# Hybrid retention / sparse attention / MoE layer on one core: the last expert's down product in its own banks, four of nine final tiles summed by TensorE

## What is computed

```python
def expert_block(args):
    tok, e = args
    xb = h[tok]
    hid = jax.nn.silu(xb @ w_gate[e]) * (xb @ w_up[e])
    return hid @ w_down[e]
...
x = x + hier_moe(...)          # each frame: gate_0 * row_0 + gate_1 * row_1
y = rmsnorm(x, g_final)
```

## Time and profile before

| | us |
|---|---|
| median of three runs | 1272.99 (1272.86 to 1273.10) |
| the profiled execution | 1269.63 |
| its span | 1267.8 |
| TensorE busy | 1122.5 (89%) |
| VectorE busy | 866.8 (68%) |
| ScalarE busy | 690.8 (54%) |
| GpSimd busy | 244.4 (19%) |

### The profile page before, as it was taken

How to read it: one execution, slowest core, us unless ns; L and a number is a source line. 1 busy time by engine, 2 the same in 40 slices (tenths; PEclk the granted TensorE clock), 3 DMA queues, 4 the chain that set the end, 5 groups by cost and what they waited for, 6 DMA issues and landing times.

```text
span 1267.8 us, 18011 instructions
## 1 busy us (share of the span) xinstructions
PE 1122.5 (89%) x6433; PEld 938.5 (74%) x6433; DVE 866.8 (68%) x1771; ACT 690.8 (54%) x1183; POOL 244.4 (19%) x276
## 2 busy tenths in 40 slices
PE   5998889999999899999999789997699999999920
PEld 4985477887878897888988468885578888888810
DVE  6529868787878777433242533356899999999847
ACT  6347578686868333243433432113378888888622
POOL 1320033324342200000000000000233433433213
PEclk8999999999999999999999899998799999999965
DMA  8352030404030232432423625103599999999656
GB/s 275 45 118 26 29 96 1 109 1 108 1 86 1 57 106 82 109 87 79 118 59 102 222 65 198 50 34 133 216 402 400 392 388 397 386 398 391 243 214 254
DMA packets 129536, 205.35 MB, mean 162 GB/s; under 512 B 17396, under 2 KB 102804, under 8 KB 117156
## 3 DMA queue, kind: packets, MB, share of 16 engines
q1 hardware_dynamic: 114852, 177.61, 40.4%
q0 software_dynamic: 12864, 21.02, 5.3%
q10 hardware_dynamic: 1728, 5.51, 1.1%
HBM read 182.03 MB, written 34.37 MB: 171 GB/s over the span
## 4 chain that ended last, share of the span: by engine, by line
PE 76%; DVE 13%; ACT 3%; issue 3%; DMA 2%; SPq 1%; POOL 0%; DVEq 0%; POOLq 0%; ACTq 0%
PE psum L2186 5%; PE psum L2188 5%; PE psum L2187 5%; PE psum L2461 4%; PE psum L2459 4%; PE psum L2460 4%; DVE place L1440 3%; PE psum L2334 3%; PE psum L2336 3%; PE psum L2335 3%; PE psum L2159 3%; PE psum L2161 2%; PE psum L2160 2%; PE psum L2476 2%; PE psum L2478 2%
## 5 line engine op out<-in xcount | busy, mean ns | idle before, releaser
L1858 DVE TENSOR_TENSOR place<-place,place 128x2048 fp32r<-128x2048 f32 x64 | 146.2, 2286 | 8.4 <-ACT place L1246 8.4
L1071 ACT ACTIVATE place<-place,place 128x768 uint8<-128x768 f32 (+3 forms) x128 | 125.5, 983 | 6.8 <-DVE place L1471 6.8
L2186 PE MATMUL psum<-place,place 128*128 128x512 f32 x288 | 123.7, 430 | 3.0 <-DVE place L1427 2.9
L1246 ACT CAST place<-place 128x2048 fp32r<-128x2048 f32 x64 | 122.2, 1912 | 0.0
L2188 PE MATMUL psum<-place,place 128*128 128x512 f32 x288 | 114.2, 397 | 0.0
L2187 PE MATMUL psum<-place,place 128*128 128x512 f32 x288 | 113.9, 396 | 0.0
L2459 PE MATMUL psum<-place,place 128*128 128x512 f32 x256 | 107.1, 418 | 0.0
L2461 PE MATMUL psum<-place,place 128*128 128x512 f32 x256 | 102.2, 399 | 0.0
L2460 PE MATMUL psum<-place,place 128*128 128x512 f32 x256 | 101.2, 395 | 0.0
L2159 PE MATMUL psum<-place,place 128*128 128x256 f32 x288 | 86.9, 302 | 3.5 <-ACT place L1093 3.5
L882 POOL TENSOR_TENSOR place<-place,place 128x1 f32<-128x1 f32 x9 | 5.1, 566 | 428.4 <-DVE place L1818 428.4
(11 more groups left out here) (324 smaller groups left out, 3111.1 us busy)
## 6 DMA issues: line engine op xcount, KB each, us to landing
place<-in_w_gate SPq DMA_DIRECT2D x32, 1024.0 KB
place<-in_w_up SPq DMA_DIRECT2D x32, 1024.0 KB
place<-in_w_down SPq DMA_DIRECT2D x32, 1024.0 KB, 10.7
place<-in_w_in SPq DMA_DIRECT2D x28, 512.0 KB, 6.4
place<-expert_out SPq DMA_DIRECT2D x9, 1024.0 KB, 13.0
place<-in_cache_attn_k SPq DMA_DIRECT2D x32, 256.0 KB, 3.2
place<-in_cache_attn_v SPq DMA_DIRECT2D x32, 256.0 KB, 3.4
place<-in_x_prompt SPq DMA_DIRECT2D x3, 1536.0 KB, 6.8
```

What stands on the lines that cost most here:

```text
L1071: last = nc.scalar.activation(reached[j], score[j], ACT.Sign, bias=pivot.bitcast(F32)[:, j:j + 1], scale=-1.0, accum_out=minus[:, j - BY_A ...
L1246: nc.scalar.copy(w_gu_hi[e % 2][:, :, ks, :], w_gu[e % 3][:, :, ks, :]).then_inc(w_hi_done, 1)
L1858: nc.vector.tensor_tensor(w_gu_lo[e % 3][:, :, ks, :], w_gu[e % 3][:, :, ks, :], w_gu_hi[e % 2][:, :, ks, :].bitcast(F32), ALU.subtract).t ...
L2186: nc.tensor.matmul(bank(4 + b), hT_hi[:, k, rows], w_hi[:, k, :], start=k == 0, stop=False)
```

## The change

The last expert's `down` writes banks 2 and 3 and no longer waits for `rows_out(30)`. Its weights are rounded and their remainder is formed one turn ahead on both engines. TensorE does the transposes `hidden(31)` between the two halves of `down(30)`. Then four of the nine final tiles (1, 3, 5, 7) are summed by TensorE in PSUM: identity times `x1` plus two products with diagonal matrices that hold the gates, which ScalarE writes beforehand. The tiles are finished in the order 0, 2, 1, 4, 3, 6, 5, 7, 8, and the normed tile is written over the first half of its own loaded rows instead of one of three buffers. The loads still go out in the order 0 to 8.

```diff
+ON_PE, LAST_ORDER = (1, 3, 5, 7), (0, 2, 1, 4, 3, 6, 5, 7, 8)
...
-        out_rows = [take(D) for _ in range(3)]
+        gate_diagonal = [[place(xT_at + 3 * D + P * (2 * n + j), P) for j in range(2)] for n in range(len(ON_PE))]
+        out_rows = [rows[:, 0, :] for rows in y_in]
...
+        def down_bank(e):
+
+            return 6 if e < NE - 1 else 2
...
+        def x2_after(x):
+
+            return sum(0 if t in ON_PE else 2 for t in LAST_ORDER[:x + 1])
...
-                nc.scalar.copy(y_rows[e % 2][:, 0:512], bank(6)).then_inc(y_act, 1)
+                nc.scalar.copy(y_rows[e % 2][:, 0:512], bank(down_bank(e))).then_inc(y_act, 1)
...
             for e in range(NE):
                 if e + 1 < NE:
                     rows_hi(e + 1)
+                else:
+                    down_hi(e)
...
                 gate_silu(e)
-                down_hi(e)
+                if e + 1 < NE:
+                    down_hi(e)
+                else:
+                    hidden_hi(e)
                 if e >= 1:
                     rows_out(e - 1)
-            hidden_hi(NE - 1)
             rows_out(NE - 1)
+            for n, t in enumerate(ON_PE):
+                for j in range(2):
+                    nc.scalar.activation(gate_diagonal[n][j], ident, ACT.Copy, scale=gates[:, j, t:t + 1]).then_inc(mix_hi_done, 1)
...
+            for x in range(T + 1):
+                if x < T:
+                    t = LAST_ORDER[x]
+                    if t in ON_PE:
+                        act.wait_ge(wo_ps, T + ON_PE.index(t) + 1)
+                        rows = bank(2 * ON_PE.index(t), 0, D)
+                    else:
+                        act.wait_ge(x2_done, x2_after(x))
+                        rows = x1[:, t, :]
+                    act.wait_ge(ssq_done, 2 * T + x)
+                    nc.scalar.activation(squared, rows, ACT.Square, accum_out=ssq7[:, x:x + 1]).then_inc(ssq_done, 1)
+                if x >= 1:
+                    t = LAST_ORDER[x - 1]
+                    act.wait_ge(out_done, x)
+                    act.dma_start(y_p[t * P:(t + 1) * P, :] if t < TP else y_s, out_rows[t]).then_inc(y7_out[(x - 1) % 3], 16)
...
-                nc.vector.tensor_scalar(y_rows[e % 2][:, 512:D], bank(7), 1.0, None, ALU.mult).then_inc(y_dve, 1)
+                nc.vector.tensor_scalar(y_rows[e % 2][:, 512:D], bank(down_bank(e) + 1), 1.0, None, ALU.mult).then_inc(y_dve, 1)
...
+                if e == NE - 1:
+                    down_lo(e)
                 hidden(e)
                 if e == 1:
                     over_blocks()
-                down_lo(e)
+                if e + 1 < NE:
+                    down_lo(e)
+                else:
+                    hidden_lo(e)
                 if e >= 1:
                     rows_out(e - 1)
-            hidden_lo(NE - 1)
             rows_out(NE - 1)
...
+            for x in range(T + 1):
+                if x < T and LAST_ORDER[x] not in ON_PE:
+                    t = LAST_ORDER[x]
                     v.wait_ge(*y_loaded(t))
                     for j in range(2):
                         nc.vector.scalar_tensor_tensor(x1[:, t, :], y_in[t][:, j, :], gates[:, j, t:t + 1], x1[:, t, :], ALU.mult, ALU.add).then_inc(x2_done, 1)
-                        v.wait_ge(x2_done, 2 * t + j + 1)
-                if t >= 1:
-                    s = t - 1
-                    v.wait_ge(rstd_done, 2 * T + t)
-                    if s >= 3:
-                        v.wait_ge(y7_out[s % 3], 16 * (s // 3))
-                    nc.vector.scalar_tensor_tensor(out_rows[s % 3], x1[:, s, :], rstd7[:, s:s + 1], g_final, ALU.mult, ALU.mult).then_inc(out_done, 1)
-                if t < T:
-                    v.wait_ge(ssq_done, 2 * T + t + 1)
-                    nc.vector.tensor_scalar(ssq7[:, t:t + 1], ssq7[:, t:t + 1], 1.0 / D, EPS, ALU.mult, ALU.add).then_inc(ms_done, 1)
+                        v.wait_ge(x2_done, x2_after(x) - 1 + j)
+                if x >= 1:
+                    t = LAST_ORDER[x - 1]
+                    v.wait_ge(rstd_done, 2 * T + x)
+                    rows = bank(2 * ON_PE.index(t), 0, D) if t in ON_PE else x1[:, t, :]
+                    nc.vector.scalar_tensor_tensor(out_rows[t], rows, rstd7[:, x - 1:x], g_final, ALU.mult, ALU.mult).then_inc(out_done, 1)
+                if x < T:
+                    v.wait_ge(ssq_done, 2 * T + x + 1)
+                    nc.vector.tensor_scalar(ssq7[:, x:x + 1], ssq7[:, x:x + 1], 1.0 / D, EPS, ALU.mult, ALU.add).then_inc(ms_done, 1)
...
-                if e >= 1:
+                if 1 <= e < NE - 1:
                     pe.wait_ge(y_act, e)
                     pe.wait_ge(y_dve, e)
                 for half_n in range(2):
-                    cols = slice(512 * half_n, 512 * half_n + 512)
+                    cols, to = slice(512 * half_n, 512 * half_n + 512), bank(down_bank(e) + half_n)
+                    if e == NE - 2 and half_n == 1:
+                        hidden(NE - 1)
                     for k in range(2):
                         hi, lo = w_dn_hi[e % 2][:, k, cols], w_dn_lo[e % 3][:, k, cols]
-                        nc.tensor.matmul(bank(6 + half_n), hidT_hi[e % 2][:, k, :], hi, start=k == 0, stop=False)
-                        nc.tensor.matmul(bank(6 + half_n), hidT_hi[e % 2][:, k, :], lo, start=False, stop=False)
-                        last = nc.tensor.matmul(bank(6 + half_n), hidT_lo[e % 2][:, k, :], hi, start=False, stop=k == 1)
+                        nc.tensor.matmul(to, hidT_hi[e % 2][:, k, :], hi, start=k == 0, stop=False)
+                        nc.tensor.matmul(to, hidT_hi[e % 2][:, k, :], lo, start=False, stop=False)
+                        last = nc.tensor.matmul(to, hidT_lo[e % 2][:, k, :], hi, start=False, stop=k == 1)
                 last.then_inc(dn_ps, 1)
...
                     down(e - 1)
-            hidden(NE - 1)
             down(NE - 1)
+            pe.wait_ge(y_act, NE)
+            pe.wait_ge(y_dve, NE)
...
+            pe.wait_ge(mix_hi_done, T + 2 * len(ON_PE))
+            for n, t in enumerate(ON_PE):
+                pe.wait_ge(*y_loaded(t))
+                for m in range(2):
+                    cols, to = slice(512 * m, 512 * m + 512), bank(2 * n + m)
+                    nc.tensor.matmul(to, ident, x1[:, t, cols], start=True, stop=False)
+                    for j in range(2):
+                        last = nc.tensor.matmul(to, gate_diagonal[n][j], y_in[t][:, j, cols], start=False, stop=j == 1)
+                last.then_inc(wo_ps, 1)
```

More of the change, by code:

```diff
@@ L1318, in _ @@
             y_p, y_s = o_["y_p"].rearrange("a s d -> (a s) d"), o_["y_s"].rearrange("b s d -> (b s) d")
-            for t in range(T + 1):
-                if t < T:
-                    act.wait_ge(x2_done, 2 * (t + 1))
-                    nc.scalar.activation(squared, x1[:, t, :], ACT.Square, accum_out=ssq7[:, t:t + 1]).then_inc(ssq_done, 1)
-                if t >= 1:
-                    s = t - 1
-                    act.wait_ge(out_done, s + 1)
-                    act.dma_start(y_p[s * P:(s + 1) * P, :] if s < TP else y_s, out_rows[s % 3]).then_inc(y7_out[s % 3], 16)
+            for x in range(T + 1):
[13 more added lines that the diff above has]
+                    act.dma_start(y_p[t * P:(t + 1) * P, :] if t < TP else y_s, out_rows[t]).then_inc(y7_out[(x - 1) % 3], 16)
             for n in range(3):
```

## The result

| | before | after |
|---|---|---|
| median of four runs each, one chip | 1272.92 (1271.39 to 1273.10) | 1262.89 (1262.22 to 1265.15) |
| ratio, 95% interval | | 0.9934 [0.9918, 0.9950] |
| profiled execution, its span | 1269.63, 1267.8 | 1262.55, 1260.7 |

The kernel is 0.5% to 0.8% faster. The forecast of 7.1 us is a ratio of 0.9944, inside the interval; the time forecast, 1265.9, is 3.0 us above the median, which lies 0.6 us under the lower end of the range.

A forecast was written before the change was run, and what follows sets the result against it. It took a serial chain up to 1224.1 (last product, scatter, load), then VectorE's nine tiles, as the bound; 4.3 us before the loads plus 2.8 after made 7.1, 1272.99 to 1265.9, range 1263.5 to 1269.8.

The forecast's parts named there:

- The last product: Expert 31's down product: no pause, clock stays 1.00, ends at 1209.65 instead of 1214.01; 4.3 us, bounds 2.5 to 4.5.
- only the pause goes: Lower case for expert 31's down product: TensorE's wait ahead of it disappears, without the clock's gain; 2.5 us.
- The way to the loads: After expert 31's product: copy out, scatter of 3.51 us and load of 4.96 us move unchanged; tile 0 lands at 1219.8.
- The final tiles: After the loads: TensorE takes eight of VectorE's eighteen sums; tile 7's sum ends at 1247.0; 2.8 us saved.
- the roots open for 0.66 us: VectorE's final tiles: waits for the inverse root, 0.66 us, four times (tiles 2, 4, 6 and 5).
- The span: Whole profiled kernel: from 1267.8 to 1260.7, 7.1 us less, 4.3 before the loads and 2.8 after.
- From the profiled execution to the median: Whole kernel: median taken 3.36 us above the profiled execution; 1272.99 - 7.1 = 1265.9.
- The clock falls before tile 7: Rival at TensorE's fourth sum: half rate costs 1.7 to 5.1 us, giving 1267.6 to 1271.0; chance 0.17.
- The loads give it back: Rival at the final loads: paired stores delay tile 7 by 1.25 us each, two make 1268.4; chance 0.10.
- The clock never rises: Rival at TensorE's final sums: clock stays 0.50, tile 7 ends at 1263.7; 9.6 us slower, 1282.6; chance 0.05.
- The early split doesn't work: Rival at expert 31's weights: remainder misses its gap, product still waits; about 4 us less, 1270; chance 0.04.
- More than forecast: Better case at the final loads: tile 7 lands sooner, floor set by tile 8; 10.3 us, 1262.7; chance 0.08.

The follow-up runs named there:

- banks_only: Kernel before, with the last down product in banks 2 and 3 without waiting for expert 30's copy out, plus two new TensorE waits; split and transposes unmoved: ratio 1.0003.
- tiles_only: Kernel before plus only the final-tile edits (TensorE sums, new order, writing over loaded rows) and the two new TensorE waits: ratio 0.9986.
- whole_change: The changed kernel timed once more beside the kernel before: ratio 0.9946.
- warm: Changed kernel with 15 extra TensorE products, results unused, before the first final tile to have the clock up: ratio 1.0004 to the kernel before.
- stores_on_sp: Changed kernel with the nine final stores issued by SP behind all loads instead of by ScalarE: ratio 0.9945 to the kernel before.
- three_on_pe: Changed kernel with tile 7 summed by VectorE again, TensorE summing only tiles 1, 3 and 5: ratio 0.9949 to the kernel before.

## Why the prediction was right, point by point

**The last product** (4.3 us, bounds 2.5 to 4.5): 4.36 in the pair of profiles. The reasons hold too: no pause, clock 1.00 through the product, the weights' remainder in VectorE's gap, the rounded hidden rows ready before TensorE needed them. The term isn't a constant, though. 1.6 of its 4.3 us is a fall of the clock after the pause, which `banks_only` did not have after the same pause; an execution of before without it, if there are such, leaves 2.8 us, just above the lower bound that I gave for "only the pause goes".

**The way to the loads.** I took the scatter's 3.51 us as moving with the rest. It took 4.51 after, and the time from scatter to load 0 was 3.57 to 4.96 us over all profiles, with before at the low end. That cost 1.0 us in this pair. How much of it is the change's isn't shown: the change puts the last two scatters 2.8 us apart instead of 5.7, and the ten profiles with its whole first half have 4.15 to 4.96 us (mean 4.6), the other four 3.57 to 4.77 (mean 4.2).

**The final tiles** (2.8 us): 2.0 in the pair, 3.0 in `tiles_only`, 2.1 in `whole_change`. The mechanism was right to a tenth: tile 1's sum in 7 to 8.7 us took 7.5, tile 7 waited for its data up to 1.7 us and did so for 1.34, the sum ended at 1247.1 (forecast 1247.0), and the end followed as computed. The term that was mis-sized is tile 7's landing behind tile 0, 22.66 us where I took before's 21.86. Two details: the roots open for 0.66 us were the four that I named and the last tile's, and VectorE was through with tile 5 at 1245.4, a little earlier than I counted.

**The span** of 1260.7 was hit exactly, and this is chance. The landing of tile 0 came 0.8 us earlier than forecast (hidden rows 1.7 early, scatter 1.0 late), that of tile 7 behind it 0.8 later. The sum in us of the two mechanisms is what the forecast can claim, not the digit.

**From the profiled execution to the median.** This is the step that put the median under the range. I added the 3.36 us by which before's median stood above its profiled execution. After's stands 0.34 above its own. Before's profiled execution was a quick one among runs that spread from 1268.5 to 1275.4 in a later measurement, and the offset says something of that execution alone. The medians of the first pair lie 10.0 us apart, those of before and `whole_change`, measured later, 7.8, against a forecast of 7.1. Taken against the ratio, whose interval holds 0.9944, and against the later 0.9946, the forecast stands.

**The rivals.** *The clock falls before tile 7*: no, 1.00 in the stretch of tile 7. The Trainium skill ("TensorE: Matmul & The Clock Gate", section "HAM oscillation — how this bites in real kernels") tells of a kernel in which waits for DMA of about 3 to 5 us between bursts of products made every burst start at the low clock. This case's trace agrees where the wait is longer than those: tile 1, behind 14.65 us, started at 1.2 GHz. Tile 7's wait of 1.34 us is shorter than those, and the section doesn't say that such a wait costs the clock. *The loads give it back*: tile 7 came at 20.7 to 22.5 us behind tile 0 in the four kernels with before's tiles, and at 20.8 to 22.7 in the five with the change's order and stores (`warm`, whose sums and stores ran late, left out); the means are 21.8 and 21.9, so the pairs of stores cost nothing that can be told from the spread. *The clock never rises*: it rose 4.2 us after tile 1's sum began. *The early split doesn't work*: it does, by the 5.36 us from hidden rows to copy. *More than forecast*: not by an earlier tile 7; where stores were moved so that it came 3.6 to 3.8 us earlier, TensorE became the bound instead, which I hadn't counted when I set that case's floor by tile 8 alone.

## What to carry to other kernels

Work given to an idle engine is worth only what the next bound allows: compute the end once along each chain (here tile 7's landing + 19.07 us, TensorE's back-to-back sums, VectorE's list) and take the latest; order the slow starter's tiles so that the busy engine has a sum of its own in front of each result it waits for. For a pause in a matmul chain look at which list holds the last input back, since here moving the weight split one turn ahead, and the transposes with it, gave the gain that freeing the banks alone did not. And before adding the difference between one profiled execution and a median, look at how far executions of one kernel lie apart.

## What the runs showed of the hardware that I had not expected

- The granted clock after a pause of 2.5 us on TensorE: 0.50 in before, 1.00 in `banks_only`, with the same products on both sides. After 1.34 us with full transfer traffic: 1.00. From the start of sums at 1.2 GHz to 2.4 GHz it took 4.2 us in after, 5.8 us in `stores_on_sp` and 6.0 in `three_on_pe`.
- 7.6 to 8.1 us of TensorE without a product where its list waits 0.7 us for a copy and then passes a loop that does no work, 3.9 us of it (in `warm`) in one branch.
- GpSimd's inverse root of one column took 0.55 us when VectorE was waiting for it and 1.52 us when VectorE was at a sum; the timeline of after shows both for line 944:

```profile
1241.50 0.55 POOL L944 TENSOR_TENSOR place<-place,place 128x1 f32<-128x1 f32 x1 [3.60 <-DVE place L2005]
1243.51 0.55 POOL L944 TENSOR_TENSOR place<-place,place 128x1 f32<-128x1 f32 x1 [1.46 <-DVE place L2005]
1248.50 1.52 POOL L944 TENSOR_TENSOR place<-place,place 128x1 f32<-128x1 f32 x1 [4.44 <-DVE place L2005]
```

The row at 1248.50 is tile 7's root, during VectorE's sums of tile 8 at 1248.34; the others stand where VectorE had nothing else to do.
